# Attention by head pairs: scores on row halves, probabilities divided before they are turned, the product with v in column halves

## The chip, the cores and the metric

One core of one Trainium2 chip runs the whole program. The metric is the device time of one execution in microseconds (us); lower is better. All data is float32.

## The reference, cut to what matters

The program is one inference step of a hybrid model with two trunk layers over 640 tokens: 128 context tokens and 512 latent tokens. Each layer projects its input, mixes tokens in three branches (an RWKV-7 scan, a convolution, attention), merges them by gates and ends with an expert look-up. The change touches the attention branch alone. There are 8 query heads of width 64 and 2 key/value heads; heads 0 to 3 use the first, 4 to 7 the second.

```python
def block_attention(q, k, v):
    ...
    scale = HEAD_DIM ** -0.5
    def one_block(q_blk):
        s = jnp.einsum('bqhgd,bkhd->bhgqk', q_blk, k).astype(jnp.float32) * scale
        p = jax.nn.softmax(s, axis=-1)
        return jnp.einsum('bhgqk,bkhd->bqhgd', p.astype(v.dtype), v)
```

The context tile of 128 queries sees 128 keys; each of the four latent tiles of 128 queries sees 640 keys (512 latent ones and 128 from the cache).

## The kernel before, in words

The kernel is a loop over two layers, and each layer is a row of stages; every stage is a block in which each engine has its own list of instructions, and the next stage starts when all engines have ended. Engines meet by counting semaphores: `Marks` turns a name such as `exp7` into the count to wait for. Names: TensorE is PE, VectorE is DVE, ScalarE is ACT.

`attention_stage` (L679) works in 40 units, a unit being one tile `i` (0 is the context tile, 1 to 4 the latent ones) and one head `h`. A float32 matmul is issued as two passes (two records); a transpose is one. For each unit PE does, in this order (L767 to L795):

- it turns the unit's probabilities, one 128x128 transpose per block of 128 keys (L773): 5 in a latent tile, 1 in tile 0;
- it does a share of the gate products (L780), which belong to the merge stage and are put here to fill PE: 3 matmuls of 128x512 in heads 0, 1, 3 and 4, 2 of them in heads 2 and 5, and 8 of 128x128 in heads 6 and 7;
- it mixes with v (L791): the turned probabilities (128 columns) are the stationary side and v (64 columns) the moving one, 5 matmuls that add up in `mixed_bank`, with the queries on the partitions;
- it makes the scores of the unit two ahead (L753, L754, in tile 0 L756): contraction over 64 rows, the moving side 512 and 128 columns wide.

DVE takes each row's largest score from PSUM (`bound`, L804) and turns it into the exponential's bias (L806), copies the turned probabilities to SBUF (L833), and in between shifts the inputs of another branch (`shift_lora`, L817 and L819). ACT does the exponential with its row sum (L865), copies the fifth turned block (L876) and empties the gate products after heads 2, 5 and 7 (`empty_gates`, L856, L858). After head 7 of a tile DVE divides the mixed result by the row sums into `y` (L838, L841); PE turns `y` in `turn_y` (L762), one head later, and DVE copies it into `y_attn` (L810). SP stores the emptied gates (L735) and waits at the end for those stores.

Elsewhere, the wkv stage has matmuls on halves of the rows. `gram_of` (L1270, L1271) has 64 contraction rows; `HEAD_ORDER` gives the two directions opposite row halves. Each of its calls issues L1270 and then L1271, both in two passes, for one direction, and then the other direction's call follows. L1403 and L1405 use the array's quarters on the diagonal (rows 0 to 63 with columns 0 to 63, and the same with 64 to 127), and `cross` (L1314) for direction 0 the quarter of rows 0 to 63 with columns 64 to 127, each with its own stationary and moving data.

## Time and profile before

| | us |
|---|---|
| median of 3 executions | 6249.18 |
| lowest, highest | 6248.24, 6256.7 |
| span of the profiled execution, first to last instruction | 6240.7 |
| attention, layer 1: first score product to last gate product | 375.9 to 576.3 |
| attention, layer 2 | 3488.7 to 3689.1 |

The profile gives its execution's span only; the median lies 8.5 us above it, and what is outside the span has no rows. A row of a timeline gives the start and the length in us; for a merged row the count stands behind `x`.
### The profile page before, as it was taken

The numbers are of one execution on the slowest core, as the hardware profiler recorded it, in microseconds if no ns is written. First come the engines' busy times: TensorE is split into PE (matmuls) and PEld (weight loads), VectorE is DVE, ScalarE is ACT, GpSimd is POOL, SyncE is SP. The second block draws the span as 40 slices with busy tenths as digits, with TensorE's granted clock in tenths as the row PEclk, the third lists the DMA queues.
The fourth block names the chain that finished last, engine by engine and source line by source line (L and its number), as shares of the span: only waits on it lengthen the run. The fifth ranks groups of instructions, "written<-read, shape, count | busy, mean of one in ns | idle before, by whom it ended". The sixth has DMA issues, their size and how long they took to land. (4 is left out here: it accounts for less than half of the span.)

```text
span 6240.7 us, 68974 instructions
## 1 busy us (share of the span) xinstructions
PE 5243.8 (84%) x25836; PEld 2768.9 (44%) x25836; DVE 3778.2 (61%) x8459; ACT 1315.2 (21%) x3140; POOL 1500.1 (24%) x1408
## 2 busy tenths in 40 slices
PE   7989899997987777777789898999978877777777
PEld 3555588543333333333345555885433333333332
DVE  3544666526677777777635446664267777777775
ACT  1022311202222222222110222112022222222221
POOL 0100000002444444444301000000033444444443
PEclk9999999998999999999999999999989999999999
DMA  3212610427999999999831125105179999999998
GB/s 126 70 69 96 225 51 29 183 84 288 420 420 419 411 418 408 418 413 413 372 111 68 69 112 209 51 29 196 71 318 420 420 419 410 419 408 418 407 420 359
DMA packets 327767, 1664.20 MB, mean 267 GB/s; under 512 B 36201, under 2 KB 69225, under 8 KB 161793
## 3 DMA queue, kind: packets, MB, share of 16 engines
q0 software_dynamic: 193504, 1370.70, 53.4%
q1 hardware_dynamic: 133920, 289.01, 12.7%
q8 instruction: 206, 3.38, 0.2%
q14 instruction: 137, 1.11, 0.0%
HBM read 1585.80 MB, written 73.79 MB: 266 GB/s over the span
## 5 line engine op out<-in xcount | busy, mean ns | idle before, releaser
L2126 PE MATMUL psum<-peer_rows,peer_diagonal 128*128 128x512 f32 x5120 | 2493.5, 639 | 692.9 <-ACT peer_diagonal L2173 692.9
L2078 POOL DMA_INDIRECT peer_rows<-in_peer_rows,look_up_index x1280 | 1431.1, 1118 | 3317.9 <-PE psum L2126 1748.1
L2240 DVE CUSTOM_DVE_ANT_0 peer_rows<-peer_rows,h_rows 128x1024 f32<-128x1024 f32 x1280 | 1547.0, 1224 | 837.9 <-DMA peer_rows<-in_peer_rows,look_up_index 834.8
L2126 PEld LDWEIGHTS psum<-peer_rows,peer_diagonal 128*128 128x128 f32 x5120 | 1009.0, 203 | 2095.4 <-issue 1193.9
L2173 ACT ACTIVATE peer_diagonal<-ident_sb,peer_weight 128x128 f32<-128x128 f32 x1280 | 409.6, 390 | 700.3 <-DVE peer_weight L2212 700.3
L2167 ACT ACTIVATE peer_active<-peer_dots 128x4 f32<-128x4 f32 x324 | 66.5, 205 | 1641.4 <-DVE peer_dots L2240 1641.4
L468 PE MATMUL psum<-in_weights,h_sb 128*128 128x512 f32 (+1 forms) x800 | 309.9, 549 | 0.0
L984 PE MATMUL psum<-h_sb,rw_in_gate_weights 128*128 128x512 f32 (+1 forms) x768 | 214.2, 440 | 26.0 <-DMA rw_in_gate_weights<-in_w_gate 26.0
L468 PEld LDWEIGHTS psum<-in_weights,h_sb 128*128 128x128 f32 x800 | 152.0, 190 | 158.1 <-issue 154.0
L961 POOL DMA_DIRECT2D rw_in_gate_weights<-in_w_gate x24 | 14.2, 594 | 864.5 <-DMA scratch_rkv_scratch<-rkv_staged 658.1
L521 DVE SCALAR_TENSOR_TENSOR conv_acc<-conv_in,conv_taps,conv_acc 128x655 f32<-128x655 f32 x240 | 216.4, 902 | 8.5
L1405 PE MATMUL psum<-wkv_inverse,wkv_inner 64*64 64x64 f32 x3200 | 193.2, 228 | 27.8 <-DVE wkv_inner L1599 27.6
L472 PE MATMUL psum<-h_sb,in_weights 128*128 128x128 f32 (+1 forms) x704 | 194.5, 440 | 4.0 <-PEq L248 4.0
L804 DVE TENSOR_REDUCE attention_largest<-psum 128x1 f32<-128x640 f32 (+1 forms) x80 | 57.4, 717 | 226.9 <-PE psum L754 186.8
L1610 DVE TENSOR_TENSOR wkv_inverse<-wkv_inverse,psum 128x512 f32<-128x512 f32 (+1 forms) x200 | 123.9, 631 | 117.1 <-PE psum L1405 115.7
L780 PE MATMUL psum<-h_sb,gate_weights 128*128 128x128 f32 (+1 forms) x640 | 191.1, 442 | 0.0
L1405 PEld LDWEIGHTS psum<-wkv_inverse,wkv_inner 64*64 64x64 f32 x3200 | 168.0, 143 | 36.0 <-DVE wkv_inner L1599 36.0
L1403 PE MATMUL psum<-wkv_inner,wkv_inverse 64*64 64x64 f32 x2560 | 172.6, 230 | 8.2 <-DVE wkv_inner L1599 8.2
L984 PEld LDWEIGHTS psum<-h_sb,rw_in_gate_weights 128*128 128x128 f32 x768 | 119.3, 193 | 125.7 <-issue 99.3
L1403 PEld LDWEIGHTS psum<-wkv_inner,wkv_inverse 64*64 64x64 f32 x2560 | 146.1, 143 | 18.8 <-DVE wkv_inner L1599 9.6
L472 PEld LDWEIGHTS psum<-h_sb,in_weights 128*128 128x128 f32 x704 | 108.7, 196 | 88.3 <-issue 88.3
L2087 PE MATMUL psum<-h_sb,query_weights 128*128 128x512 f32 x256 | 134.6, 608 | 9.6 <-PEq L1933 9.6
(356 smaller groups left out, 6153.0 us busy)
## 6 DMA issues: line engine op xcount, KB each, us to landing
rw_out_mod_weights<-in_w_mod SPq DMA_DIRECT2D x16, 2048.0 KB
in_weights<-in_w_in SPq DMA_DIRECT2D x12, 2048.0 KB, 8.5
peer_rows<-in_peer_rows,look_up_index POOLq DMA_INDIRECT x1280, 16.7
modulation_weights<-in_w_mod SPq DMA_DIRECT2D x8, 2048.0 KB
scratch_rw_scratch<-rw_in_direction SPq DMA_DIRECT2D x20, 768.0 KB, 6.9
wkv_own<-scratch_rw_scratch SPq DMA_DIRECT2D x20, 768.0 KB, 6.7
rw_in_gate_weights<-in_w_gate POOLq DMA_DIRECT2D x24, 512.0 KB, 6.2
scratch_rw_scratch<-rw_in_z SPq DMA_DIRECT2D x10, 1024.0 KB, 5.8
```

The lines of the kernel that those rows point to most:

```text
L468: last = nc.tensor.matmul(t.bank[n % BANKS][:, 0:width(n)], t.h[:, k, i * P:(i + 1) * P], weights[c % 2][:, k, 0:chunks[c][1]], start=(k = ...
L472: last = nc.tensor.matmul(t.bank[n % BANKS][:, 0:m], weights[c % 2][:, k, i * P:(i + 1) * P], t.h[:, k, lo:lo + m], start=(k == 0), stop=( ...
L521: convolved.step(nc.vector.scalar_tensor_tensor(out=out, in0=t.conv_in[:, j, k:k + CONV_SPAN], scalar=taps[:, j, k:k + 1], in1=out, op0=AL ...
L780: last = nc.tensor.matmul(out, t.gate_weights[:, place, k, :], t.h[:, k, lo:lo + m], start=(k == 0), stop=(k == KD - 1))
L984: last = nc.tensor.matmul(out[:, 0:m], gate_weights[b % 2][:, k, :], t.h[:, k, lo:lo + m], start=(k == 0), stop=(k == KD - 1))
L1403: mm(banks(d)[1][rows, h * HB:(h + 1) * HB], inverse[n % 2][d][rows, 1, h, :], inner[d][rows, h, :], start=True, stop=True)
L1405: last = mm(banks(d)[1][rows, (4 + h) * HB:(5 + h) * HB], inner[d][rows, h, :], inverse[n % 2][d][rows, 1, h, :], start=True, stop=True)
L2078: nc.gpsimd.indirect_dma_start(rows[spot][:, :], None, t.dram["peer_rows"], bass.IndirectOffsetOnAxis(ap=index[j % 4][:, k:k + 1], axis=0) ...
L2087: last = nc.tensor.matmul(query_bank, t.query_weights[:, k, j * P:(j + 1) * P], t.h[:, k, CTX:NTOK], start=(k == 0), stop=(k == KD - 1))
L2126: last = nc.tensor.matmul(t.bank[2 * (i % 2) + c], diagonal[k % DIAGONALS][:, :], rows[spot][:, D + c * 512:D + (c + 1) * 512], start=(j = ...
L2173: nc.scalar.activation(diagonal[k % DIAGONALS][:, :], t.ident[:, :], ACT.Identity, scale=weight[b][:, k:k + 1]).then_inc(s["diagonal"], 1)
L2240: v.tensor_tensor_reduce(rows[spot][:, 0:D], rows[spot][:, 0:D], h[:, :], 1.0, 0.0, ALU.mult, ALU.add, dots[b][:, k:k + 1]).then_inc(s["do ...
```

## The change

The 40 units become 20 rounds `r`, a round being a tile and a pair of heads `p` with members `e` = 0 and 1.

- `scores(r)` makes both heads' scores, alternating between rows 0 to 63 and 64 to 127, into two separate pairs of banks. They are made one round ahead.
- `divide` (DVE) takes the reciprocal of one head's row sums and multiplies the 128x640 probabilities by it before they are turned. The division of the mixed result, `y` and `turn_y` are gone.
- `turn(r, e)` writes four blocks into a bank of its own for each `e`, and the fifth into a free part of a score bank; so `scores(r + 1)` waits until ACT has copied that fifth block (`copied{r}_1`).
- `mix(r)` has v (64 columns) stationary and the turned probabilities (128 columns) moving. Head `e` writes partitions 64e to 64e + 63 of `mixed_bank`, the two heads alternating block by block. The result is y already turned, and DVE copies it to `y_attn`.
- On PE a round is: turn 0, turn 1, gates of the first head, scores of the next round, gates of the second head, mix.
- `shift_lora` runs in rounds 5, 7, 9, 11, 13 and 15, after `prepare` of the next round.

```diff
@@ block.tensor @@
-            scores(0)
-            scores(1)
-            for u, (i, h) in enumerate(units):
-                pe.wait_ge(s["scalar"], SCALAR.after(f"exp{u}"))
...
-                for j in range(blocks_of(i)):
-                    v = t.cached_v[:, at:at + HD] if j == 4 else t.qkv[:, j + (i > 0), 640 + at:640 + at + HD]
-                    last = nc.tensor.matmul(mixed_bank[:, h * HD:(h + 1) * HD], probs_turned[u % 2][:, j * P:(j + 1) * P], v,
-                                            start=(j == 0), stop=(j == blocks_of(i) - 1))
+            def scores(r):
+                i, p = rounds[r]
+                if r:
+                    pe.wait_ge(s["scalar"], SCALAR.after(f"copied{r - 1}_1" if rounds[r - 1][0] else f"exp{r - 1}_1"))
+                for lo, hi in ((0, 512), (512, NK)) if i else ((0, P),):
+                    for e in range(2):
+                        rows, v = slice(e * HD, e * HD + HD), 0 if p // 2 == e else 1
+                        at = P if i else 0
+                        last = nc.tensor.matmul(scores_of[e][:, lo:hi], t.q_turned[rows, p, i * P:(i + 1) * P], t.keys[rows, v, at + lo:at + hi],
+                                                start=True, stop=True)
+                last.then_inc(s["tensor"], 1)
+            def turn(r, e):
+                i, _ = rounds[r]
+                pe.wait_ge(s["vector"], VECTOR.after(f"scaled{r}_{e}"))
+                for j in range(blocks_of(i)):
+                    out = turned_last[e] if j == 4 else turned_banks[e][:, j * P:(j + 1) * P]
+                    last = nc.tensor.transpose(out, probs[e][:, j * P:(j + 1) * P], t.ident[:, :])
+                last.then_inc(s["tensor"], 1)
+            def mix(r):
+                i, p = rounds[r]
+                at = p // 2 * HD
+                pe.wait_ge(s["vector"], VECTOR.after(f"copied{r}_1"))
+                if i:
+                    pe.wait_ge(s["scalar"], SCALAR.after(f"copied{r}_1"))
+                    if p == 0:
+                        pe.wait_ge(s["vector"], VECTOR.after(f"y_copied{i - 1}"))
+                for j in range(blocks_of(i)):
+                    v = t.cached_v[:, at:at + HD] if j == 4 else t.qkv[:, j + (i > 0), 640 + at:640 + at + HD]
+                    for e in range(2):
+                        last = nc.tensor.matmul(mixed_bank[e * HD:e * HD + HD, p * P:(p + 1) * P], v, probs_turned[e][:, j * P:(j + 1) * P],
+                                                start=(j == 0), stop=(j == blocks_of(i) - 1))
+                last.then_inc(s["tensor"], 1)
+            scores(0)
+            for r in range(ROUNDS):
+                turn(r, 0)
+                turn(r, 1)
+                gates(r, 0)
+                if r + 1 < ROUNDS:
+                    scores(r + 1)
+                gates(r, 1)
+                mix(r)
@@ block.vector @@
+            def divide(r, e):
+                i, p = rounds[r]
+                h, n = 2 * p + e, blocks_of(i) * P
+                dve.wait_ge(s["scalar"], SCALAR.after(f"exp{r}_{e}"))
+                nc.vector.reciprocal(inverse[:, h:h + 1], total[:, h:h + 1]).then_inc(s["vector"], 1)
+                dve.wait_ge(s["vector"], VECTOR.after(f"inverse{r}_{e}"))
+                nc.vector.tensor_scalar(probs[e][:, 0:n], probs[e][:, 0:n], inverse[:, h:h + 1], None, ALU.mult).then_inc(s["vector"], 1)
+            def prepare(r):
+                for e in range(2):
+                    bound(r, e)
+                for e in range(2):
+                    divide(r, e)
@@ block.scalar @@
+            for r, (i, p) in enumerate(rounds):
+                for e in range(2):
+                    if i:
+                        act.wait_ge(s["tensor"], TENSOR.after(f"turned{r}_{e}"))
+                        nc.scalar.copy(probs_turned[e][:, 4 * P:NK], turned_last[e]).then_inc(s["scalar"], 1)
+                    if e == 1 and r + 1 < ROUNDS:
+                        for ahead in range(2):
+                            exponentials(r + 1, ahead)
+                    if 2 * p + e in GATE_HEADS:
+                        empty_gates(i, GATE_HEADS.index(2 * p + e))
```

PE before, heads 1 and 2 of the first latent tile (`psum<-a,b` lists what is read; the shape is what is written):

```order
L773 MATMUL psum<-ident_sb,attention_probs 128x128 x5
L780 MATMUL psum<-h_sb,gate_weights 128x512 x3
L791 MATMUL psum<-qkv,attention_probs_turned 128x64 x4
L791 MATMUL psum<-cached_v,attention_probs_turned 128x64
L753 MATMUL psum<-keys,q_turned 128x512
L754 MATMUL psum<-keys,q_turned 128x128
L773 MATMUL psum<-ident_sb,attention_probs 128x128 x5
L780 MATMUL psum<-h_sb,gate_weights 128x512 x2
L791 MATMUL psum<-qkv,attention_probs_turned 128x64 x4
L791 MATMUL psum<-cached_v,attention_probs_turned 128x64
L753 MATMUL psum<-keys,q_turned 128x512
L754 MATMUL psum<-keys,q_turned 128x128
```

PE now, the pair of heads 4 and 5 of that tile:

```order
L763 MATMUL psum<-ident_sb,attention_probs 128x128 x10
L774 MATMUL psum<-h_sb,gate_weights 128x512 x3
L754 MATMUL psum<-keys,q_turned 128x512 x2
L754 MATMUL psum<-keys,q_turned 128x128 x2
L774 MATMUL psum<-h_sb,gate_weights 128x512 x2
L789 MATMUL psum<-attention_probs_turned,qkv 64x128 x8
L789 MATMUL psum<-attention_probs_turned,cached_v 64x128 x2
```

Two units of four steps have become one round in which the score and mixing products of both heads stand together, with the gate products between them; v is now the stationary side of the last two rows.

DVE before, two units of the first latent tile:

```order
L833 COPY attention_probs_turned<-psum 128x512
L804 TENSOR_REDUCE attention_largest<-psum 128x1
L806 TENSOR_SCALAR attention_bias<-attention_largest 128x1
L833 COPY attention_probs_turned<-psum 128x512
L804 TENSOR_REDUCE attention_largest<-psum 128x1
L806 TENSOR_SCALAR attention_bias<-attention_largest 128x1
```

DVE now, one round of that tile:

```order
L833 COPY attention_probs_turned<-psum 128x512 x2
L811 TENSOR_REDUCE attention_largest<-psum 128x1
L813 TENSOR_SCALAR attention_bias<-attention_largest 128x1
L811 TENSOR_REDUCE attention_largest<-psum 128x1
L813 TENSOR_SCALAR attention_bias<-attention_largest 128x1
L820 RECIPROCAL attention_inverse<-attention_total 128x1
L822 TENSOR_SCALAR attention_probs<-attention_probs,attention_inverse 128x640
L820 RECIPROCAL attention_inverse<-attention_total 128x1
L822 TENSOR_SCALAR attention_probs<-attention_probs,attention_inverse 128x640
```

The two copies stand first, and two reciprocals and two 128x640 multiplications have come in behind the two bounds, ahead of the next copies.

ACT now, from the exponentials ahead of the pair of heads 2 and 3 to those ahead of the next pair (L892 copies the fifth block, L874 empties the gate product of head 2):

```order
L883 ACTIVATE attention_probs,attention_total<-psum,attention_bias 128x640 x2
L892 COPY attention_probs_turned<-psum 128x128
L874 COPY y_rw<-psum 128x512
L892 COPY attention_probs_turned<-psum 128x128
L883 ACTIVATE attention_probs,attention_total<-psum,attention_bias 128x640 x2
```

The emptying of head 2's gates now stands between the two copies of fifth blocks, and so ahead of the one that `scores(r + 1)` waits for.

## Rows read from the trace of the kernel before

**Rows 1.** The page's head: span of the profiled execution.

```profile
span 6240.7 us, 68974 instructions
```

**Rows 2.** Busy by stretch: attention in both layers, up to the last gate product.

```profile
core 0: us, PE busy (x) PEld busy (x) DVE busy (x) ACT busy (x) POOL busy (x), PEclk, DMA share, GB/s
375.90:576.30 200.40, 196.21 (x975) 130.70 (x976) 71.11 (x153) 45.59 (x127) 0.00 (x0) 0.98 0.07 27
...
3488.70:3689.10 200.40, 196.23 (x974) 130.64 (x975) 71.12 (x153) 45.60 (x127) 0.00 (x0) 0.98 0.07 27
```

**Rows 3.** Timeline of head 2 of the first latent tile: start us, length us, engine, line.

```profile
417.18 0.77 PE L773 MATMUL psum<-ident_sb,attention_probs 128*128 128x128 f32 x5
417.29 0.82 DVE L804 TENSOR_REDUCE attention_largest<-psum 128x1 f32<-128x640 f32 x1 [2.90 <-PE psum L754]
...
417.78 1.88 PE L780 MATMUL psum<-h_sb,gate_weights 128*128 128x512 f32 x4
...
418.40 0.79 ACT L865 ACTIVATE attention_probs<-psum,attention_bias 128x640 f32<-128x640 f32 x1 [4.57 <-DVE attention_bias L806]
...
419.09 0.19 ACT L865 ACTIVATION_READ_ACCUMULATOR attention_probs<-psum,attention_bias 128x1 f32 x1
419.18 0.26 ACT L876 COPY attention_probs_turned<-psum 128x128 f32<-128x128 f32 x1
...
419.50 1.09 PE L791 MATMUL psum<-qkv,attention_probs_turned 128*128 128x64 f32 x8
419.70 0.58 ACT L856 COPY y_rw<-psum 128x512 f32<-128x512 f32 x1 [0.27 <-PE psum L780]
...
420.75 1.12 PE L753 MATMUL psum<-keys,q_turned 64*128 64x512 f32 x2
...
422.02 0.76 PE L773 MATMUL psum<-ident_sb,attention_probs 128*128 128x128 f32 x5
```

**Rows 4.** Timeline of PE in the wkv stage: products on 64 rows, two directions.

```profile
770.78 0.71 PE L1270 MATMUL psum<-wkv_turned 64*128 64x256 f32 x4
771.31 0.60 PE L1271 MATMUL psum<-wkv_turned 64*128 64x256 f32 x4
```

**Rows 5.** Timeline of PE there: L1403 and L1405 beside L1314.

```profile
791.02 0.22 PE L1403 MATMUL psum<-wkv_inner,wkv_inverse 64*64 64x64 f32 x2
...
791.08 0.22 PE L1403 MATMUL psum<-wkv_inner,wkv_inverse 64*64 64x64 f32 x2
...
791.14 0.22 PE L1314 MATMUL psum<-wkv_u,h_sb 64*64 64x64 f32 x1
...
791.20 0.22 PE L1314 MATMUL psum<-wkv_u,h_sb 64*64 64x64 f32 x1
```

**Rows 6.** Groups by line and shape, VectorE.

```profile
L2233 DVE RECIPROCAL peer_inverse<-peer_total 128x1 f32<-128x1 f32 x80 | 12.5, 156 | 4.2 <-ACT h_rows L2149 4.2
...
L817 DVE TENSOR_SCALAR inputs_ahead<-lora,attention_mu_lora_own 128x512 f32<-128x512 f32 x6 | 2.9, 478 | 0.0
...
L817 DVE TENSOR_SCALAR inputs_ahead<-lora,attention_mu_lora_own 128x128 f32<-128x128 f32 x6 | 1.7, 277 | 0.0
```

**Rows 7.** Timeline: two units of the context tile, and turn_y with what follows.

```profile
382.97 0.33 PE L773 MATMUL psum<-ident_sb,attention_probs 128*128 128x128 f32 x1
...
386.39 0.33 PE L773 MATMUL psum<-ident_sb,attention_probs 128*128 128x128 f32 x1
...
408.71 0.60 PE L762 MATMUL psum<-ident_sb,attention_y 128*128 128x128 f32 x4
...
409.14 1.00 PE L791 MATMUL psum<-qkv,attention_probs_turned 128*128 128x64 f32 x8
```

**Rows 8.** Timeline of the stage's end, first layer.

```profile
576.87 0.36 SPq L735 DMA_DIRECT2D scratch_gate_scratch<-y_rw  x1
...
580.40 0.74 ACT L1013 ACTIVATE inputs_ahead<-inputs_ahead 128x640 f32<-128x640 f32 x1 [3.56 <-PEq L696]
```

**Rows 9.** Waits in the latent tiles, first layer: us, times, longest.

```profile
PE psum L791 <- DVE attention_probs_turned L833: 2.6, 3, 1.5
```

More of the change, by code:

```diff
@@ L682, in attention_stage @@
     NK = 5 * P
-    UNITS = TILES * HEADS
-    units = [divmod(u, HEADS) for u in range(UNITS)]
-    tensor_order, vector_order, scalar_order = ["scores0", "scores1"], ["max0", "bias0", "max1", "bias1"], ["exp0"]
-    for u, (i, h) in enumerate(units):
-        ahead = u + 2 < UNITS
-        tensor_order += [f"turned{u}"] + [f"y_turned{i - 1}"] * (h == 0 and i > 0) + [f"mixed{u}"] + [f"scores{u + 2}"] * ahead
-        vector_order += [f"copied{u}"] + [f"y_copied{i - 1}"] * (h == 0 and i > 0)
-        vector_order += [f"inverse{i}", f"y{i}"] * (h == HEADS - 1) + [f"max{u + 2}", f"bias{u + 2}"] * ahead
-        scalar_order += [f"exp{u + 1}"] * (u + 1 < UNITS) + [f"copied{u}"] * (i > 0)
-    TENSOR = Marks(*tensor_order, f"y_turned{TILES - 1}")
+    ROUNDS = TILES * PAIRS
+    rounds = [divmod(r, PAIRS) for r in range(ROUNDS)]
+    bounds = [f"{what}{{0}}_{e}" for e in range(2) for what in ("max", "bias")] + [f"{what}{{0}}_{e}" for e in range(2) for what in ("inverse", "scaled")]
+    tensor_order, vector_order, scalar_order = ["scores0"], [name.format(0) for name in bounds], ["exp0_0", "exp0_1"]
+    for r, (i, p) in enumerate(rounds):
+        ahead = r + 1 < ROUNDS
+        tensor_order += [f"turned{r}_0", f"turned{r}_1"] + [f"scores{r + 1}"] * ahead + [f"mixed{r}"]
+        vector_order += [f"copied{r}_0"] + [f"y_copied{i - 1}"] * (p == 0 and i > 0) + [f"copied{r}_1"]
+        vector_order += [name.format(r + 1) for name in bounds] * ahead
+        scalar_order += [f"copied{r}_0", f"copied{r}_1"] * (i > 0) + [f"exp{r + 1}_0", f"exp{r + 1}_1"] * ahead
+    TENSOR = Marks(*tensor_order)
     VECTOR = Marks(*vector_order, f"y_copied{TILES - 1}")
@@ L759, in turn_y @@
-            def turn_y(i):
-                pe.wait_ge(s["vector"], VECTOR.after(f"y{i}"))
-                for j in range(PAIRS):
-                    last = nc.tensor.transpose(y_bank[:, j * P:(j + 1) * P], y[:, j * P:(j + 1) * P], t.ident[:, :])
-                last.then_inc(s["tensor"], 1)
-            scores(0)
-            scores(1)
-            for u, (i, h) in enumerate(units):
-                pe.wait_ge(s["scalar"], SCALAR.after(f"exp{u}"))
-                if i and h == 1:
-                    pe.wait_ge(s["vector"], VECTOR.after(f"y_copied{i - 1}"))
-                for j in range(blocks_of(i)):
-                    out = turned_last[:, 0:P] if j == 4 else turned_bank[:, j * P:(j + 1) * P]
-                    last = nc.tensor.transpose(out, probs[u % 2][:, j * P:(j + 1) * P], t.ident[:, :])
-                last.then_inc(s["tensor"], 1)
+            def scores(r):
[8 more added lines that the diff above has]
+                                                start=True, stop=True)
+                last.then_inc(s["tensor"], 1)
@@ L808, in copy_y, with copy_turned @@
+            def prepare(r):
[3 more added lines that the diff above has]
+                    divide(r, e)
+            def copy_turned(r, e):
+                n = 4 * P if rounds[r][0] else P
+                dve.wait_ge(s["tensor"], TENSOR.after(f"turned{r}_{e}"))
+                nc.vector.tensor_copy(probs_turned[e][:, 0:n], turned_banks[e][:, 0:n]).then_inc(s["vector"], 1)
             def copy_y(i):
-                dve.wait_ge(s["tensor"], TENSOR.after(f"y_turned{i}"))
@@ L820, in shift_lora @@
                                                                 op0=ALU.mult, op1=ALU.add))
[L822 to L823 removed]
+            prepare(0)
             dve.wait_ge(s["mu_loaded"], 16)
@@ L859, in empty_gates, with exponentials @@
                                    ).then_inc(s["gate_emptied"], 1)
[L861 to L878 removed]
+            def exponentials(r, e):
+                i, p = rounds[r]
+                h, n = 2 * p + e, blocks_of(i) * P
+                act.wait_ge(s["vector"], VECTOR.after(f"bias{r}_{e}"))
+                nc.scalar.activation(probs[e][:, 0:n], scores_of[e][:, 0:n], ACT.Exp, bias=bias[:, h:h + 1],
+                                     scale=scale, accum_out=total[:, h:h + 1]).then_inc(s["scalar"], 1)
+            for e in range(2):
+                exponentials(0, e)
+            for r, (i, p) in enumerate(rounds):
+                for e in range(2):
+                    if i:
[6 more added lines that the diff above has]
+                        empty_gates(i, GATE_HEADS.index(2 * p + e))
             act.wait_ge(s["gate_emptied"], 3 * TILES)
```

97 lines of the change are left out of this document (28 added, 69 removed).

## The prediction

> **What bounds the kernel now.** I read the span first [rows 1], then the attention stretches. From the first score product to the last gate product both layers take 200.4 us, and PE is busy for 196.2 of it while DVE has 71 and ACT 46 [rows 2]. So in this stage PE is the bound; what its list of instructions gets shorter by is gained, unless a new wait opens. Outside the stage nothing changes. The timeline of one latent unit shows where PE's time goes [rows 3]: turning 417.18 to 417.78, gates to 419.50, mixing to 420.75, scores to the next unit's 422.02. That is 0.60, 1.72, 1.25 and 1.27 us. The gates stay: two matmuls are four passes, so a 512-wide pass takes 0.43 us, 0.83 ns a column, and by the same pace a 128-wide pass 0.107 and a 64-wide one 0.053. The mixing's ten passes stand 0.11 apart although their moving side has only 64 columns: there the 128-column weight load is the limit, and it is what the swap of sides removes.
>
> **Do two halves run beside each other?** For rows, the wkv stage shows it [rows 4]. The two directions call with opposite row halves; four L1270 passes and then four L1271 passes of 256 columns start within 0.98 us (770.78 to 771.76, where the next L1270 could begin), while eight after each other would take 8 x 0.213 = 1.71. All four L1270 come before the first L1271, though each direction's list has two L1270 and then its own two L1271: the halves are fed apart. So both heads' scores take the time of one. The skill's page "TensorE: Matmul & The Clock Gate", Part 3, says that matmuls start strictly in program order; the trace disagrees, and what that rule would cost is a rival below. For columns there is no row of the changed shape, 128 rows by 64 columns. The nearest [rows 5]: L1403's two diagonal quarters go on at 0.06 a pass (791.02, 791.08) while L1314, which shares its rows with one of them and its columns with the other, goes at 0.06 too (791.14, 791.20). So two column halves with the same rows should run together. The bounds for the 20 passes of one latent mix (two heads, five blocks, two passes) are 10 x 0.107 = 1.07 if they do and 20 x 0.107 = 2.14 if they don't. I take 1.07, by rows 5.
>
> **PE, part by part, for one layer** (16 latent rounds instead of 32 units; the stage is measured up to the last gate product).
> - Turning: 32 x 0.60 before; now ten transposes in a row at 0.11 are 1.1 a round: 19.2 - 17.6 = **1.6**.
> - Scores: 32 x 1.27 = 40.6 (two of them issued in tile 0). Now 16 x 1.42, the 1.27 of one head plus 0.15, since they now stand between gate products, whose exposed weight load and emptying of the array cost a little more than before a transpose. 40.6 - 22.7 = **17.9**.
> - Mixing: before the last gate product lie 31 x 1.25 = 38.8. Now 15 x 1.33, 1.07 of stream, 0.05 for the first 64-column load and about 0.2 for the changes of form on both sides: 38.8 - 20.0 = **18.8**. An estimate for the changes of form: the score part's 1.27 holds 0.85 + 0.21 = 1.07 of stream, which leaves 0.2. Bounds for one change are 0 and 0.2; with four in a round, as before, that is 3 us a layer either way.
> - `turn_y`: 408.71 to 409.14 [rows 7], four times: **1.7**. The fifth lies behind the last gate product.
> - Tile 0: a unit takes 386.39 - 382.97 = 3.42, less six gate passes 2.56 leaves 0.86, for a pair 1.72. Now 0.22 of transposes, 0.21 + 0.36 for scores and 0.21 + 0.26 for mixing: 1.26, times three and a half pairs: **1.6**.
> - Waits of the mixing for the turned copy, behind `shift_lora`, 2.6 us in three waits [rows 9]: gone, since a round leaves the copies a gate part and a score part (over 3 us). **2.6**.
>
> **What it adds.** On DVE, 40 reciprocals (0.156) and 40 multiplications; their price by L817, SBUF to SBUF with a scalar per row: 0.28 at 128 columns and 0.48 at 512 give 0.54 at 640 [rows 6]. Bounds: 0.48, the 512-wide row itself, and 0.82, the 640-wide reduction from PSUM [rows 3]. That is 25 us on an engine with 129 us idle, but it lies in the chain from scores to turning. From the reduction's start: the exponential starts at +1.11, its sum is there at +1.99 [rows 3]; the second head's reduction and bias end at +1.9, its exponential runs from +2.04 to +2.92; then reciprocal and multiplication: the first head's probabilities are ready at +2.74, the second's at +3.65. The reduction starts 0.2 after the scores, so 2.95 and 3.85 after them. PE has between: gates of the second head (2.56, or 1.72 in two rounds of four), mix 1.33, and 0.2: 3.25 at the least, and 0.55 more before the second head is turned, 3.8. It just covers; I cost it at nothing. If the multiplication took 0.82, PE would wait 0.4 behind the gates of heads 5 and 7, 3 us a layer. `shift_lora` (up to 2.0 us) makes the next copies late, but the first thing behind those copies is the mix, more than 5 us later.
>
> Two costs are certain. At the start both divisions come before the first gates: 2 x (0.16 + 0.28) = **-0.9**. And in the second round of every latent tile ACT has the emptying of head 2's gates between the two copies of the fifth blocks, while the next scores wait for the second copy. The unit in rows 3 has the same pieces: gates end 419.50, emptying starts 419.70 and takes 0.58, a copy takes 0.26, PE goes on 0.05 after it. So PE stands 1.09, of which 0.12 would have gone into the change of form: 4 x 0.97 = **-3.9**. The stage's tail gains nothing: the last gate store is issued at 576.87 and the next stage begins at 580.40 [rows 8], and that store follows the last gate product as before; `y`'s division and `turn_y` lay beside it.
>
> **Sum.** 1.6 + 17.9 + 18.8 + 1.7 + 1.6 + 2.6 - 0.9 - 3.9 = 39.4 us a layer, 78.8 in two; the two layers agree to the decimal [rows 2]. The span would go from 6240.7 to 6162; the median of the runs lies 8.5 above the span, and I leave that: 6249.2 - 78.8 = **6170**. The clock is near full in the stage (0.98) and should stay there, since PE has no long gap.
>
> **Rivals.**
> 1. Row halves overlap, column halves don't, because both want the moving data of all 128 rows. For it: no row has this shape. Against: rows 5. Then 1.07 more in 32 mixes: +34, **6204**.
> 2. Passes start strictly in order, so that a head's second pass blocks the other head's first. The scores then take three and a half 512-wide slots in place of two and a half (+0.43 a round), the mix eleven slots instead of ten (+0.11): 0.54 x 32 = +17, **6187**. Against it: rows 4.
> 3. DVE and ACT become the bound of the round. Were the chain 1 us longer than worked out (4.85), PE would wait 1.05 behind the gates of heads 5 and 7 and 0.2 behind those of heads 1 and 3, whose cover is 4.65: 16 x 1.05 + 16 x 0.2 = +20, **6190**. For it: the cover is thin.
> 4. The halves share nothing, in rows or in columns: the change doesn't do what it says. Then the 1.07 of scores comes back too: +68, **6238**, within the noise of no change.
> 5. Slower. Every step from one half to the other empties the array, as a change of form does here, at 0.2: 3 such steps in the scores and 9 in the mix, 2.4 a round, plus the lost overlap 2.14: 4.5 x 32 = +145, **6315**. It is slower than before from 0.04 a step. Against it: in rows 4 and 5 steps between parts of one size cost nothing. The skill's page "TensorEngine Tiling (Array Packing)", Tiling Modes, says that changing the mode drains the engine but changing the tile does not; the trace agrees, with starts 0.06 apart in rows 5.
>
> **How the numbers follow.** The forecast has 0.72, rival 1 0.10, rival 2 0.06, rival 3 0.06, rival 4 0.03, rival 5 0.03. About 0.2% (12 us) is what a measurement of this kernel can tell from no change. Forecast and rivals 1 to 3 are faster: 0.94; rival 4 is the same: 0.03; rival 5 slower: 0.03. The forecast's own range is 6156 to 6184, from changes of form at nothing or 0.2 (6 either way), the multiplication (6), and waits at the start and behind `shift_lora`. To hold 8 in 10 it must reach rival 1: 6156 to 6208.
>
> **What would show it.** Right: the stretch to the last gate product is about 161 us in each layer; in each round the two heads' first 512-wide passes start within 0.1 us of each other; mixing passes at 0.054 on average; one wait of PE for ACT of about 1 us in each latent tile, before the scores behind head 2's gates. Wrong: mixing passes 0.107 apart (rival 1); score products of the two heads starting 0.43 apart (rival 2); PE waiting for the multiplication ahead of most turnings (rival 3); more than 0.1 between passes of different halves (rival 5).

## The result

| | before | changed |
|---|---|---|
| median, us | 6252.94 (4 executions) | 6174.7 (4 executions) |
| lowest to highest | 6248.24 to 6258.76 | 6168.82 to 6181.04 |
| span of the profiled execution | 6240.7 | 6179.3 |
| attention stage, layer 1 / layer 2, first score product to the next stage | 204.4 / 204.5 | 168.6 / 168.7 |

The ratio is 0.9877, 95% interval 0.9864 to 0.989: 1.2% faster, 78 us by the medians. Run again beside other kernels later, the changed kernel had a median of 6171.16 against 6251.35, ratio 0.9871 (0.9853 to 0.9888), and a stage of 167.3 us in layer 1 and 167.4 in layer 2.

The attention stages give 71.6 us of it in the first profile and 74.2 in the second; that is what the traces show as the change's own. In the first pair of profiles the rest of the program took 10.2 us longer (6.6 of it in the second layer's wkv stage, at a mean granted clock of 0.924 over the whole span against 0.937), in the second pair 0.0. The profiled execution of before was also a short one: in the changed kernel's runs the time is the span plus 1.7, so before's 6240.7 stands for about 6242.4, and the lowest of all times measured for it is 6243.62.

The page's head and busy times of the changed kernel, which answer to [rows 1]:

```profile
span 6179.3 us, 68906 instructions
...
PE 5219.4 (84%) x25796; PEld 2726.7 (44%) x25796; DVE 3821.1 (62%) x8599; ACT 1319.7 (21%) x3140; POOL 1491.9 (24%) x1408
```

Its stretches up to the last gate product, which answer to [rows 2], and the stage's start apart:

```profile
core 0: us, PE busy (x) PEld busy (x) DVE busy (x) ACT busy (x) POOL busy (x), PEclk, DMA share, GB/s
375.90:540.40 164.50, 158.53 (x948) 94.02 (x948) 93.06 (x224) 47.60 (x127) 0.00 (x0) 0.97 0.09 33
376.00:384.30 8.30, 6.67 (x13) 2.68 (x13) 2.40 (x12) 2.13 (x5) 0.00 (x0) 0.51 0.81 279
...
3454.30:3618.80 164.50, 158.57 (x947) 94.02 (x948) 93.06 (x224) 47.60 (x127) 0.00 (x0) 0.97 0.09 33
```

The stretch takes 164.5 us instead of 200.4 (163.3 in the second profile; 161 was forecast), and PE is still busy for 158.5 of them: it is still the bound. DVE went from 71 to 93.

One round of the first latent tile, heads 2 and 3, answers to [rows 3]:

```profile
415.50 1.31 PE L763 MATMUL psum<-ident_sb,attention_probs 128*128 128x128 f32 x10
...
416.65 1.88 PE L774 MATMUL psum<-h_sb,gate_weights 128*128 128x512 f32 x4
...
418.57 0.59 ACT L874 COPY y_rw<-psum 128x512 f32<-128x512 f32 x1 [2.00 <-PE psum L774]
419.05 0.27 ACT L892 COPY attention_probs_turned<-psum 128x128 f32<-128x128 f32 x1
...
419.38 1.35 PE L754 MATMUL psum<-keys,q_turned 64*128 64x512 f32 x8 [0.84 <-ACT attention_probs_turned L892]
...
420.66 2.84 PE L774 MATMUL psum<-h_sb,gate_weights 128*128 128x512 f32 x6
420.77 0.82 DVE L811 TENSOR_REDUCE attention_largest<-psum 128x1 f32<-128x640 f32 x1 [3.18 <-PE psum L754]
...
422.94 0.55 DVE L822 TENSOR_SCALAR attention_probs<-attention_probs,attention_inverse 128x640 f32<-128x640 f32 x1
...
423.43 1.09 PE L789 MATMUL psum<-attention_probs_turned,qkv 128*64 128x128 f32 x16
...
423.86 0.55 DVE L822 TENSOR_SCALAR attention_probs<-attention_probs,attention_inverse 128x640 f32<-128x640 f32 x1
...
424.35 0.39 PE L789 MATMUL psum<-attention_probs_turned,cached_v 128*64 128x128 f32 x4
...
424.67 1.31 PE L763 MATMUL psum<-ident_sb,attention_probs 128*128 128x128 f32 x10
```

Read the starts on PE: turning both heads 415.50 to 416.65; gates, then a wait, to 419.38; both heads' scores to 420.66, 1.28 us where one head took 1.27; gates to 423.43; the mix of both heads to 424.67, 1.24 us for twenty passes where ten took 1.25 in head 2's unit and 1.15 to 1.18 in most others. The row of the scores merges eight passes, four of each head; in the round before this one the first passes of the two heads start at 410.21 and 410.22. The multiplications of the two heads (422.94 and 423.86, 0.55 each) lie beside gates and mix.

What PE waits for in the stage (line, releaser, us in total, times, longest):

```profile
PE psum L754 <- ACT attention_probs_turned L892: 3.4, 4, 0.8
...
PE psum L763 <- DVE attention_probs L822: 2.2, 3, 1.6
```

Of the 2.2 us, 1.6 are the first turning of the stage, and the other two waits come on entering the first latent tile.

The end, which answers to [rows 8]:

```profile
541.02 0.36 SPq L734 DMA_DIRECT2D scratch_gate_scratch<-y_rw  x1
...
544.66 0.74 ACT L1032 ACTIVATE inputs_ahead<-inputs_ahead 128x640 f32<-128x640 f32 x1 [3.66 <-PEq L697]
```

From the store's issue to the next stage 3.64 us, before 3.53: the tail is the store's, as forecast.

### The profile page after: what moved, and what is told of

It reads as the page before. It is cut to its first block and busy times, and to the rows that moved or that the text cites. A ratio compares the mean times of both kernels' runs of the same rounds, so it can differ in the third digit from the quotient of the medians.

```text
span 6179.3 us, 68906 instructions
## 1 busy us (share of the span) xinstructions
PE 5219.4 (84%) x25796; PEld 2726.7 (44%) x25796; DVE 3821.1 (62%) x8599; ACT 1319.7 (21%) x3140; POOL 1491.9 (24%) x1408
## 5 line engine op out<-in xcount | busy, mean ns | idle before, releaser
L2145 PE MATMUL psum<-peer_rows,peer_diagonal 128*128 128x512 f32 x5120 | 2532.3, 648 | 654.7 <-ACT peer_diagonal L2192 650.7
L2145 PEld LDWEIGHTS psum<-peer_rows,peer_diagonal 128*128 128x128 f32 x5120 | 1031.3, 207 | 2074.5 <-issue 1236.2
L1422 PE MATMUL psum<-wkv_inner,wkv_inverse 64*64 64x64 f32 x2560 | 174.5, 232 | 5.2 <-DVE wkv_inner L1618 5.2
L1422 PEld LDWEIGHTS psum<-wkv_inner,wkv_inverse 64*64 64x64 f32 x2560 | 147.6, 145 | 15.9 <-issue 8.9
L1861 PE MATMUL psum<-merge_last_weights,merged 128*128 128x512 f32 x320 | 137.8, 593 | 3.2 <-DVE merge_product L1878 3.2
```

The costliest lines, as they stand in the source:

```text
L1422: mm(banks(d)[1][rows, h * HB:(h + 1) * HB], inverse[n % 2][d][rows, 1, h, :], inner[d][rows, h, :], start=True, stop=True)
L1861: last = nc.tensor.matmul(t.bank[n % 8][:, :], merged[:, k, i * P:(i + 1) * P], last_weights[c][:, k, :], start=(k == 0), stop=(k == KD - 1))
L2145: last = nc.tensor.matmul(t.bank[2 * (i % 2) + c], diagonal[k % DIAGONALS][:, :], rows[spot][:, D + c * 512:D + (c + 1) * 512], start=(j = ...
```

## The experiments

All compare with the changed kernel. The stage's length is taken from the traces, where it is steady, because the rest of the program moves a median by several us. It has one looseness of its own: the clock is at half (the start of the stage is at 0.51 above), and this ends either early or 3.4 us later, which is worth 1.3 us, nearly all of it in the first gate products (5.21 us in the first profile of the changed kernel, 3.97 in the second). So the changed kernel's stage is 168.6 with the late and 167.3 with the early end. Late it was in e5, e6, in e8's first layer and in the second layers of e2, e9 and e10; early in all others, the kernel before included (204.4).

| run | stage, layer 1 / 2, us | median, us | ratio to before (95%) |
|---|---|---|---|
| changed kernel | 168.6 / 168.7 | 6174.7 | 0.9877 (0.9864 to 0.989) |
| changed kernel again | 167.3 / 167.4 | 6171.16 | 0.9871 (0.9853 to 0.9888) |
| e1_empty_after_copies | 163.6 / 163.6 | 6164.33 | 0.9862 (0.9846 to 0.9878) |
| e2_mix_before_gates | 165.9 / 167.4 | 6163.99 | 0.9862 (0.9845 to 0.9878) |
| e3_both | 162.3 / 162.2 | 6161.55 | 0.9856 (0.984 to 0.9873) |
| e4_mix_by_head | 177.1 / 177.3 | 6189.91 | 0.9906 (0.9889 to 0.9922) |
| e5_scores_by_head | 168.6 / 168.7 | 6168.8 | 0.9872 (0.9856 to 0.9889) |
| e6_old_sides | 179.3 / 179.7 | 6192.64 | 0.9903 (0.9886 to 0.9919) |
| e7_no_multiply | 166.4 / 166.3 | 6165.7 | 0.9863 (0.9846 to 0.9879) |
| e8_multiply_twice | 175.0 / 174.5 | 6182.86 | 0.9889 (0.9872 to 0.9905) |
| e9_one_half_by_head | 183.2 / 184.7 | 6200.26 | 0.9919 (0.9903 to 0.9936) |
| e10_covered_order | 161.1 / 162.5 | 6159.85 | 0.9852 (0.9836 to 0.9869) |

### Where the mix's gain comes from

**e6_old_sides**: the old sides of the mix, in the new rounds.

```diff
-                for j in range(blocks_of(i)):
...
-                    for e in range(2):
-                        last = nc.tensor.matmul(mixed_bank[e * HD:e * HD + HD, p * P:(p + 1) * P], v, probs_turned[e][:, j * P:(j + 1) * P],
+                for e in range(2):
+                    for j in range(blocks_of(i)):
...
+                        h = 2 * p + e
+                        last = nc.tensor.matmul(mixed_bank[:, h * HD:(h + 1) * HD], probs_turned[e][:, j * P:(j + 1) * P], v,
```

> The mix alone goes back to the old sides: the turned probabilities (128 columns) stationary, v (64 columns) moving, one head after the other; the result stays unturned, so the turning of y is left out of the computation and y_attn holds the wrong order. Theory: 20 passes at 0.11 are 2.22 us instead of 1.24, and the change of form ahead of the mix (0.2) goes: +0.8 in each of 16 latent rounds, 12 us a layer, +25 us over the changed kernel. Rival: the gain of the change is mostly in the scores, and the old mix would have been hidden by the longer cover it gives the chain: under +10.

```profile
412.69 1.00 PE L790 MATMUL psum<-qkv,attention_probs_turned 128*128 128x64 f32 x8
...
413.75 1.06 PE L790 MATMUL psum<-qkv,attention_probs_turned 128*128 128x64 f32 x8
...
414.87 0.39 PE L763 MATMUL psum<-ident_sb,attention_probs 128*128 128x128 f32 x2
```

The mix takes 414.87 - 412.69 = 2.18 us. Against the changed kernel with the same late clock the stage is 10.7 to 11.0 longer, 0.7 in each of the 15 latent rounds whose mix lies before the last gate product (expected 12), and the median is 18 to 21 above (expected 25). That is less than the 0.94 between the two mixes for two reasons: the changes of form around the mix go (the gate products ahead of it take 2.68 instead of 2.77 and the turning behind it 1.10 instead of 1.15), and the longer mix covers the small waits behind heads 5 and 7.

**e9_one_half_by_head**: v stationary as in the change, but both heads of a round in one column half.

```diff
-                for j in range(blocks_of(i)):
...
-                    for e in range(2):
-                        last = nc.tensor.matmul(mixed_bank[e * HD:e * HD + HD, p * P:(p + 1) * P], v, probs_turned[e][:, j * P:(j + 1) * P],
+                for e in range(2):
+                    half, place = p % 2 * HD, p // 2 * 2 + e
+                    for j in range(blocks_of(i)):
...
+                        last = nc.tensor.matmul(mixed_bank[half:half + HD, place * P:(place + 1) * P], v, probs_turned[e][:, j * P:(j + 1) * P],
```

> The mix head by head as in the run that did so, but both heads of a round write the same column half (even pairs the lower, odd pairs the upper), so y's heads stand in each other's places. Theory: all of the mix's gain is the overlap of the two halves; without any, 20 passes of 0.107 plus 0.17 are 2.31 us a mix, against 1.95 by head in two halves and 1.24 block by block: +1.07 x 16 = 17 us per layer, +34 over the changed kernel and +11 over the run by head. Rival: with v stationary and 64 columns of load the passes get shorter also in one half, and it stays within 15 us of the changed kernel.

```profile
423.24 1.09 PE L790 MATMUL psum<-attention_probs_turned,qkv 128*64 128x128 f32 x8
...
424.39 1.04 PE L790 MATMUL psum<-attention_probs_turned,qkv 128*64 128x128 f32 x8
...
425.57 0.66 PE L763 MATMUL psum<-ident_sb,attention_probs 128*128 128x128 f32 x4
```

425.57 - 423.24 = 2.33 us. The stage is 183.2 with the early clock and 184.7 with the late one, 15.9 and 16.0 over the changed kernel, so 32 in both layers together; the median is 26 to 29 above. So the swap of sides alone gives nothing: without the overlap the new mix is slower than the old (2.33 against 2.18). The gain is the two column halves side by side. This is rival 1's condition made real, and its price was about right (34 against 32).

### How PE feeds the halves

**e4_mix_by_head** and **e5_scores_by_head**: the loop over the two heads goes outside the loop over blocks (mix) or widths (scores), nothing else.

```diff
-                for j in range(blocks_of(i)):
...
-                    for e in range(2):
+                for e in range(2):
+                    for j in range(blocks_of(i)):
...
```

```diff
-                for lo, hi in ((0, 512), (512, NK)) if i else ((0, P),):
-                    for e in range(2):
+                for e in range(2):
+                    for lo, hi in ((0, 512), (512, NK)) if i else ((0, P),):
```

> In the mix all ten passes of the first head are issued before the ten of the second, instead of block by block. Theory: the two column halves are fed apart from a list that PE looks into, so the passes of the second head still start early: the change is under 5 us. Rival: passes start in the order of the list, so the second head starts only with the last pass of the first: 0.96 more in each of 32 latent mixes, +31 us over the changed kernel. In between: PE looks only some records ahead, and part of the 31 comes.

> The same for the scores: four passes of the first head, then four of the second (1.07 us of stream each). Theory (fed apart): no change, under 5 us. Rival (in order): the second head's first 512-wide pass starts with the first head's last: +0.96 in each of 32 rounds, +31 us. The wkv stage had two by two passes of each half in a row and overlapped, so I expect no change here with 3 in 4.

Scores by head, PE's timeline:

```profile
418.26 1.36 PE L754 MATMUL psum<-keys,q_turned 64*128 64x512 f32 x8 [0.84 <-ACT attention_probs_turned L892]
419.55 0.70 PE L774 MATMUL psum<-h_sb,gate_weights 128*128 128x512 f32 x1
```

The eight passes take 1.29 us, as in the alternating order (1.28), and the stage is unchanged: 168.6. The second head's first pass starts 0.01 after the first head's, although three more passes of the first stand between them in the list. The mix by head:

```profile
450.20 1.15 PE L789 MATMUL psum<-attention_probs_turned,qkv 128*64 128x128 f32 x10
451.12 0.27 PE L789 MATMUL psum<-attention_probs_turned,cached_v 128*64 128x128 f32 x1
451.18 0.27 PE L789 MATMUL psum<-attention_probs_turned,qkv 128*64 128x128 f32 x1
451.23 0.27 PE L789 MATMUL psum<-attention_probs_turned,cached_v 128*64 128x128 f32 x1
...
452.15 0.33 PE L763 MATMUL psum<-ident_sb,attention_probs 128*128 128x128 f32 x1
```

It takes 452.15 - 450.20 = 1.95 us, between 1.24 (alternating) and 2.33 (one half). For 0.7 us only the first head's passes start, 0.11 apart; from about 450.91 on the two interleave, 0.05 to 0.06 apart; then the second head's rest goes alone. The second head's first weight load starts at 450.91, as the first head's seventh pass does (450.90), with three of its ten still to start. So both plain theories fall for the mix: PE neither starts in the order of the list nor takes a half's passes from anywhere in it. In both runs it went past three waiting passes of the other half, and in this one not past more; what sets that limit the runs don't show. The price by the rows is 0.71 in each of the 15 latent rounds whose mix lies before the last gate product, 10.7, less 0.5, since a longer mix covers the waits behind heads 5 (0.10) and 7 (0.04); the stage is 9.8 us longer with the early clock (177.1 against 167.3), the median 15 to 19 above.

### The chain from scores to turning

**e7_no_multiply** multiplies one column instead of 640; **e8_multiply_twice** multiplies all of them once more by 1.0.

```diff
-                nc.vector.tensor_scalar(probs[e][:, 0:n], probs[e][:, 0:n], inverse[:, h:h + 1], None, ALU.mult).then_inc(s["vector"], 1)
+                nc.vector.tensor_scalar(probs[e][:, 0:1], probs[e][:, 0:1], inverse[:, h:h + 1], None, ALU.mult).then_inc(s["vector"], 1)
```

```diff
                 nc.vector.tensor_scalar(probs[e][:, 0:n], probs[e][:, 0:n], inverse[:, h:h + 1], None, ALU.mult).then_inc(s["vector"], 1)
+                dve.wait_ge(s["vector"], VECTOR.after(f"first{r}_{e}"))
+                nc.vector.tensor_scalar(probs[e][:, 0:n], probs[e][:, 0:n], 1.0, None, ALU.mult).then_inc(s["vector"], 1)
```

> The multiplication of the probabilities is cut to one of 640 columns (the reciprocal stays); so the division is left out of the computation. Theory: PE waited for it only by 0.1 in the rounds after heads 5 and 7 and by about 0.9 on entering the first latent tile, so the stage gets 1 to 2 us shorter per layer, 2 to 4 in all. Rival: DVE and ACT bound the round more than the trace's waits tell, and 10 us or more go.

> Every head's probabilities are multiplied a second time (by 1.0), 0.57 us more on DVE for each head. Theory: the chain from scores to turning just covers, so the second head's probabilities come 1.1 later; PE waits about 1.0 more in the 8 rounds of a layer after heads 5 and 7 and 0.2 after heads 1 and 3: 9 to 10 us per layer, +19 in all. Rival: DVE is busy for 57% of the stage, so the added work lies in its idle time and under 5 us come.

Without the multiplication the stage is 0.9 us shorter (166.4 against 167.3): it costs next to nothing where it stands. The waits behind heads 5 and 7 are gone (0.5 in all), but of the 0.9 on entering the first latent tile only 0.34 is; the rest is the chain without it. With two it is 6 to 7 us longer, the median 8 to 12 above (expected 19). The timeline of the twice-multiplied kernel behind head 5's gates shows how it comes in:

```profile
433.56 0.77 PE L763 MATMUL psum<-ident_sb,attention_probs 128*128 128x128 f32 x5 [0.19 <-DVE attention_probs L824]
433.61 0.55 DVE L822 TENSOR_SCALAR attention_probs<-attention_probs,attention_inverse 128x640 f32<-128x640 f32 x1
434.20 0.49 DVE L824 TENSOR_SCALAR attention_probs<-attention_probs 128x640 f32<-128x640 f32 x1
...
434.75 0.77 PE L763 MATMUL psum<-ident_sb,attention_probs 128*128 128x128 f32 x5 [0.42 <-DVE attention_probs L824]
435.35 0.83 PE L774 MATMUL psum<-h_sb,gate_weights 128*128 128x128 f32 x6
```

PE turns the first head at 433.56 and then cannot turn the second before 434.75, just after the second multiplication ends (434.69), about 0.6 after the first head's five transposes. Turning takes 1.79 us there (433.56 to 435.35) instead of 1.25, and PE waits after the mix as well (from the mix's start to the turning 1.50 instead of 1.24): 0.8 in a round where I had 1.0. Behind heads 1 and 3, with their three gate matmuls, it adds 0.04 where I had 0.2. Eight times 0.84 is 6.7 us, as in the stage. So rival 3's condition, a chain 1 us longer, costs 13 to 14 us in both layers together and not 20. The cover is what the forecast said, nearly nothing to spare behind heads 5 and 7, and it does not help that DVE idles for a third of the stage, since the chain and not the sum of DVE's work decides.

### The wait for ACT, and the order on PE

**e1_empty_after_copies**:

```diff
                     if i:
                         act.wait_ge(s["tensor"], TENSOR.after(f"turned{r}_{e}"))
                         nc.scalar.copy(probs_turned[e][:, 4 * P:NK], turned_last[e]).then_inc(s["scalar"], 1)
+                    if e == 1 and p == 1:
+                        empty_gates(i, 0)
                     if e == 1 and r + 1 < ROUNDS:
                         for ahead in range(2):
                             exponentials(r + 1, ahead)
-                    if 2 * p + e in GATE_HEADS:
+                    if 2 * p + e in GATE_HEADS[1:]:
                         empty_gates(i, GATE_HEADS.index(2 * p + e))
```

> ACT empties head 2's gate product after both copies of the fifth blocks instead of between them. Theory: the scores of the next round no longer wait for ACT behind head 2's gates; that wait is 0.9 us in each of 8 latent tiles, so the attention stage takes 3.6 us less per layer (168.6 to 165.0) and the run about 7 us less than the changed kernel. Rival: the wait was not the order but the time the copy of the fifth block needs anyway; then PE still waits there and less than 2 us go.

```profile
415.34 1.88 PE L774 MATMUL psum<-h_sb,gate_weights 128*128 128x512 f32 x4
415.54 0.27 ACT L892 COPY attention_probs_turned<-psum 128x128 f32<-128x128 f32 x1 [0.28 <-PE psum L763]
...
417.16 0.70 PE L754 MATMUL psum<-keys,q_turned 64*128 64x512 f32 x2
417.26 0.59 ACT L874 COPY y_rw<-psum 128x512 f32<-128x512 f32 x1 [1.45 <-PE psum L774]
```

The copy of the fifth block is done before the gate products end, the scores start at 417.16, 1.82 us after the gates' start (2.73 in the changed kernel: 416.65 to 419.38), and the emptying follows. 0.91 in four tiles is 3.6 us a layer, as expected; the stage is 163.6 against 167.3 with the same early clock. The median is 7 to 10 lower.

**e2_mix_before_gates** and **e3_both** (this with the change of e1):

```diff
                 if r + 1 < ROUNDS:
                     scores(r + 1)
-                gates(r, 1)
-                mix(r)
+                    mix(r)
+                    gates(r, 1)
+                else:
+                    gates(r, 1)
+                    mix(r)
```

> PE does scores, mix, gates of the second head instead of scores, gates, mix (the last round is left). Theory: every change between full rows, row halves and column halves costs about 0.2 us of PE, and this order has three in a round instead of four: 19 rounds x 0.2 = 3.8 us less per layer (168.6 to 164.8), 7.6 in all. Rival A: the cost hangs on the weight load of the gate products, which stays the same in number: no change. Rival B: the mix now comes before the copies of the turned blocks are done, and PE waits in the rounds that begin a tile: up to 1 us in each of four, so it gives half of the gain back.

> Emptying after the copies, and the mix ahead of the second head's gates in every round but the last. Theory: the two add up, -3.6 and -1.4 us per layer by the runs before, so the stage is near 163.6 (162.4 with the early clock) and the run 10 us under the changed kernel. The second part gives 0.2 only in the rounds whose second gate part is three matmuls; in the others the chain from scores to turning is exposed by as much as the saved change of form. Rival: with the wait for ACT gone the chain is exposed more, and less than 6 us remain.

Of the 3.8 us that I expected of e2 only part came. From one turning of the second head to the next, a round with three gate matmuls for the second head takes 9.02 us instead of 9.16 and 9.17: the change of form saved, 0.15. But the rounds with fewer take what they took, 8.31 and 7.57 against 8.31 and 7.59. PE's time between scores and turning is shorter by the change saved, and where it had only just covered the chain, PE waits instead. The waits of the turning's weight loads (PEld) for the multiplication show it: 7.1 us in 16 of them, where the changed kernel has 3.2 in 4.

```profile
PEld psum L763 <- DVE attention_probs L825: 7.1, 16, 1.9
```

So the stage gains about 1.3 us instead of 3.8: eight rounds of a layer at 0.15. Its median is 7 to 11 lower, more than the 2.7 us of both stages, which shows how far a median alone can be trusted here. e3_both adds the two up: 162.3, 5.0 under 167.3, and a median 10 lower, as expected.

**e10_covered_order**: as e3_both, but heads 4 and 5 trade their gate shares, and the mix goes first only in the rounds of heads 0 to 5.

```diff
+                cuts = (0, 3, 6, 8) if h < 3 else (0, 3, 5, 8)
-                return [(gate_bank[:, 0:LAT], b % GATE_PLACES, k, GROUPS[1]) for k in range(KD)[h % 3 * 3:h % 3 * 3 + 3]]
+                return [(gate_bank[:, 0:LAT], b % GATE_PLACES, k, GROUPS[1]) for k in range(cuts[h % 3], cuts[h % 3 + 1])]
...
-                gates(r, 1)
-                mix(r)
+                if rounds[r][1] < 3:
+                    mix(r)
+                    gates(r, 1)
+                else:
+                    gates(r, 1)
+                    mix(r)
```

> As the run of both, but heads 4 and 5 trade their gate shares (two and three matmuls instead of three and two), and the mix goes ahead of the gates only in the rounds of heads 0 to 5, where the second gate part is now always three matmuls long. Theory (cover): 0.2 in 12 latent rounds plus the 0.1 of waiting behind head 5 in four, on top of the 3.6 for the order on ACT: 6.4 us per layer under the changed kernel, -13 in all, and PE's waits for the multiplication fall behind heads 0 to 5. Rival: the round's length is set by something else (the copies, the queue), and it is no better than the run of both.

```profile
PEld psum L764 <- DVE attention_probs L827: 3.2, 4, 1.9
...
PE psum L764 <- DVE attention_probs L827: 2.2, 3, 1.6
```

The waits for the multiplication are back at four, and the stage is 161.1 with the early clock in layer 1 and 162.5 with the late one in layer 2, 6.2 under the changed kernel in both (expected 6.4). The median of 6159.85 is 11 under the changed kernel on the same chip, and 1.5% under before. Against e3_both (6161.55) the medians tell nothing apart; only layer 1's stage does, where both had the early clock (161.1 against 162.3). It is the best version that was run.

## Why the prediction was right

The forecast was 6170 with a range of 6156 to 6208 and 39.4 us saved in each layer's stage; the median came to 6174.7, and the stage saved 35.8 (37.1 in the second profile). What each part of PE's list gave, from the starts in layer 1 of before and of the second profile, whose half clock ended equally early:

| part | forecast, us | measured, us |
|---|---|---|
| turning, latent tiles | 1.6 | 0.4 |
| scores, latent | 17.9 | 20.7 |
| mixing, latent | 18.8 | 18.2 |
| `turn_y` | 1.7 | 2.0 |
| gate parts in latent tiles, with their waits | 2.6 - 3.9 = -1.3 | -3.8 |
| tile 0 and the start, with the wait at its end | 1.6 - 0.9 = 0.7 | -0.4 |
| sum | 39.4 | 37.1 |

Point by point:

- *PE bounds the stage*: shown, 158.5 of 164.5 us busy.
- *Row halves side by side, fed apart*: shown, 1.28 us for both heads' scores, by e5 too. Rival 2 (strictly in order) is out for the scores; for the mix e4 shows a limit that neither had, which the alternating order never meets. The Trainium skill's page "TensorE: Matmul & The Clock Gate", Part 3, has matmuls start strictly in program order; the trace and e5 disagree.
- *Column halves side by side, taken from quarters in the wkv stage*: shown, 1.24 us for the mix; e9 prices the other case.
- *Changes of form*: mis-sized a little, and put in the wrong parts. I had all of them in scores (1.42) and mix (1.33), 0.61 a round over the 1.07 of stream in each. Scores and mix come out shorter than that, 1.28 and 1.24, but the parts around them are longer:

```profile
425.82 2.74 PE L774 MATMUL psum<-h_sb,gate_weights 128*128 128x512 f32 x6
428.49 1.35 PE L754 MATMUL psum<-keys,q_turned 64*128 64x512 f32 x8
```

  Three gate matmuls took 2.58 in before; here they take 2.67 ahead of the scores (425.82 to 428.49) and 2.77 between scores and mix (420.66 to 423.43), and turning takes 1.15 where e6, without a change ahead of it, has 1.10. Together that is 0.21 + 0.17 + 0.09 + 0.19 + 0.05 = 0.71 a round, about 0.18 for each of four changes, near my upper bound of 0.2, and 0.10 a round more than costed: 1.6 us a layer. The Trainium skill's page "TensorEngine Tiling (Array Packing)", Tiling Modes, says that a change of mode drains the engine and a change of tile does not; the trace agrees, with about 0.18 for the one and the passes of alternating halves 0.055 apart on average in the mix.
- *Mixing before*: mis-sized. I took 1.25 for each of the 31 from head 2's unit. The trace of before has 1.15 to 1.18 for most of them; the unit just before head 2's is this:

```profile
414.75 1.00 PE L791 MATMUL psum<-qkv,attention_probs_turned 128*128 128x64 f32 x8
...
415.91 1.12 PE L753 MATMUL psum<-keys,q_turned 64*128 64x512 f32 x2
```

  All 31 take 36.8, not 38.8, so there was 2.0 us less to save.
- *Entering the first latent tile*: left out. The cover of the chain there holds the mix of tile 0, which is four passes and not twenty:

```profile
405.11 0.44 PE L789 MATMUL psum<-attention_probs_turned,qkv 128*64 128x128 f32 x4
...
406.01 0.76 PE L763 MATMUL psum<-ident_sb,attention_probs 128*128 128x128 f32 x5 [0.47 <-DVE attention_probs L822]
...
406.94 0.77 PE L763 MATMUL psum<-ident_sb,attention_probs 128*128 128x128 f32 x5 [0.16 <-DVE attention_probs L822]
```

  The mix starts at 405.11 and the turning only at 406.01, and its second head at 406.94: 0.9 us more than in the next rounds. I had worked out the cover for latent rounds alone.
- *The start*: the two divisions came in ahead of the first turnings and gates as costed (from the first score product to the first gate product 3.05 us instead of 2.09). The first gate products then ran for 5.21 us instead of 4.21, since the half clock ended 3.4 us later in that execution; in the second profile they took 3.97.
- *The wait for ACT behind head 2*: 0.91 instead of 0.97, shown by e1.
- *The chain just covers*: nearly. PE waits 0.10 behind each head 5 and 0.04 behind each head 7, 0.5 a layer that I had put at nothing; the multiplication took 0.55 where I had 0.54.
- *The tail*: as forecast, 3.64 us of store.
- *Lost time in before's stage*: too low. I took off 2.6 us of waits. By the starts the waits ahead of four mixes come to 3.6, and another 1.6 goes where the clock fell to half for 3.4 us (466.7 to 470.1), after PE had stood 1.47 us for DVE's copy:

```profile
464.85 1.08 PE L791 MATMUL psum<-qkv,attention_probs_turned 128*128 128x64 f32 x8 [1.47 <-DVE attention_probs_turned L833]
...
467.93 1.33 PE L773 MATMUL psum<-ident_sb,attention_probs 128*128 128x128 f32 x5
```

```profile
466.00:472.00 6.00, 6.00 (x17) 3.39 (x17) 1.67 (x3) 1.04 (x3) 0.00 (x0) 0.72 0.00 0
```

  The second view is PE's clock by stretch: 0.72 from 466 to 472. Layer 2 has the same wait and the same fall of the clock (3579.6 to 3583.1; 0.72 from 3578 to 3584). The changed kernel has neither: after the stage's start its clock stays at full. So the change gave back some 2.7 us a layer that the sum didn't have. That the wait brought the clock down is not shown.

So the mechanism held, and the total came near because terms that I had too favourable (about 5 us a layer, and 1.3 more where the half clock ended late) met the 2.7 us that I had missed. The forecast of the whole came nearer still, 78.8 against 78.2 by the medians, but the traces put only 71.6 to 74.2 in the two stages, and the interval of the ratio reaches from 69 to 85 us. That nearness is luck, not a merit of the sum. One number of the rivals was wrong by its own rows: rival 5 is slower than before from 0.03 a step and not 0.04 ((79 / 32 - 2.14) / 12).

## What to carry to other kernels

Where two products have half the rows or half the columns of the array, issue them in turn, pass by pass, with their data in opposite halves: here that brought about 2.5 us down to 1.25 twice a round, while swapping the sides alone gained nothing. Each change between full array and halves cost 0.15 to 0.2 us here, part of it in the products before and behind, so count them, and put halves of either kind next to one another only where the time between them is not what hides another engine's chain. Price a repeated part from several of its instances and not from one. When PE gets faster, work out for every round of the loop, the one across tiles too, how long the chain through the other engines is and what lies beside it.

## What was not expected of the hardware

PE goes past passes for one half that cannot start yet to those for the other half, but only past a few: four in a row cost nothing (scores by head, 1.29 against 1.28 us), ten in a row cost 0.71 us, and the second head began with three of the first still to start. What sets the limit is not shown. And the half clock at the stage's start ended 3.4 us sooner or later, from one profile to the next of the same kernel and, in some runs, from one layer to the other, worth 1.3 us of the stage.
